# Two transformer blocks on one core: dilated masks added by VectorE with row extremes stored as they come, rope tables computed at FF1's last unit, and the gate stage in another order

## The reference, cut to what matters

```python
# first layer, second half
h = rmsnorm(x, g_pre_mlp)
ff = square(relu(h @ w_ff1)) @ w_ff2             # 1024 -> 4096 -> 1024
x = x + rmsnorm(ff, g_post_mlp)
# second layer
h = rmsnorm_2(x, norm1_g); proj = h @ w_in
for g, (window, dilation) in enumerate(((128, 1), (512, 4), (2048, 16))):
    q, k = partial_rope(q_g, positions), partial_rope(k_g, positions)
    # rope: x1*cos - x2*sin, x2*cos + x1*sin on 16 of 64 features
    s = (q * 64**-0.5) @ k.T  within a residue class, own and previous 128 rows
    s = where(mask, s, -inf)
    m = max(s); p = exp(s - m); den = sum(p)
    lse = m + log(den); o = (p @ v) / den
alpha = softmax(stack(lse)); attn = sum(alpha * outs)
z = gelu(uv); u, v = split(z); v = layernorm(v, ln_g, ln_b)
sgu = u * (tril(w_s) @ v + b_s)                  # per chunk of 128 rows, 8 groups
merged = gate_a * (attn @ w_proj_attn) + gate_b * (sgu @ w_proj_sgu)
x = x + merged @ w_out                           # then norm, gated feed-forward, norm
```

## Time and profile before

| what | value |
|---|---|
| device time, median of 3 runs | 3655.24 us (3654.55 to 3655.67) |
| profiled execution, its own time | 3656.55 us |
| its span | 3654.6 us |
| PE busy | 3512.3 us (96%) |
| PE weight loads (beside it) | 2903.1 us (79%) |
| DVE busy | 1421.5 us (39%) |
| POOL busy | 987.5 us (27%) |
| ACT busy | 933.8 us (26%) |

### The profile page before, as it was taken

The page is one execution under the profiler, slowest core; times in us unless marked ns, Lnnn a source line. Parts: engine busy times, 40 slices in busy tenths (PEclk is TensorE's granted clock), DMA queues, the critical chain, the costliest instruction groups (busy, mean ns, idle before and its releaser), DMA issues.

```text
span 3654.6 us, 44410 instructions
## 1 busy us (share of the span) xinstructions
PE 3512.3 (96%) x17467; PEld 2903.1 (79%) x17467; DVE 1421.5 (39%) x2268; ACT 933.8 (26%) x1575; POOL 987.5 (27%) x429
## 2 busy tenths in 40 slices
PE   7899999999998999999799999998999999999999
PEld 6688877888776888888678888887787778888887
DVE  6882452123345333333644455444113213122234
ACT  4233443312242111111333333333322221111112
POOL 1452102223214333333312222211323122332322
PEclk9999999999999999999999999999999999999999
DMA  4232012212221111111221212213122111111111
GB/s 130 59 85 85 19 52 72 66 52 75 104 81 52 46 57 46 46 46 46 69 85 47 64 46 64 65 45 110 52 75 98 46 52 47 46 56 47 46 46 58
DMA packets 203977, 226.86 MB, mean 62 GB/s; under 512 B 19224, under 2 KB 177604, under 8 KB 203340
## 3 DMA queue, kind: packets, MB, share of 16 engines
q1 hardware_dynamic: 178556, 169.85, 15.3%
q10 hardware_dynamic: 20912, 44.54, 3.5%
q0 software_dynamic: 4384, 10.74, 0.8%
HBM read 191.30 MB, written 31.69 MB: 61 GB/s over the span
## 4 chain that ended last, share of the span: by engine, by line
PE 86%; DVE 5%; issue 5%; POOL 2%; ACT 1%; DMA 0%; ACTq 0%; SPq 0%; DVEq 0%; POOLq 0%
PE ps L274 18%; PE ps L319 16%; PE ps L301 13%; PE ps L302 13%; PE ps L295 12%; PE ps L724 4%; PE ps L2639 2%; PE ps L2610 1%; POOL wlo L266 1%; PE ps L335 1%; PE ps L2627 1%; PE ps L2123 1%; DVE big L470 1%; PE ps L2104 1%; PE ps L500 1%
## 5 line engine op out<-in xcount | busy, mean ns | idle before, releaser
L266 POOL TENSOR_TENSOR wlo<-raw,whi 128x2048 fp32r<-128x2048 f32 (+1 forms) x162 | 700.6, 4325 | 1748.0 <-ACT whi L258 1747.2
L301 PE MATMUL ps<-h_lo,whi 128*128 128x512 f32 x1856 | 723.5, 390 | 2.1 <-POOL wlo L266 2.0
L302 PE MATMUL ps<-h_hi,wlo 128*128 128x512 f32 x1856 | 723.0, 390 | 0.0
L258 ACT ACTIVATE whi<-raw 128x2048 fp32r<-128x2048 f32 (+1 forms) x162 | 288.4, 1780 | 962.0 <-PE ps L295 597.8
L295 PE MATMUL ps<-h_hi,whi 128*128 128x512 f32 x1856 | 462.1, 391 | 9.1 <-DVE gu L2783 5.3
L295 PEld LDWEIGHTS ps<-h_hi,whi 128*128 128x128 f32 x1856 | 349.6, 189 | 83.0 <-issue 9.7
L301 PEld LDWEIGHTS ps<-h_lo,whi 128*128 128x128 f32 x1856 | 349.3, 188 | 76.0 <-POOL wlo L266 3.3
L302 PEld LDWEIGHTS ps<-h_hi,wlo 128*128 128x128 f32 x1856 | 349.0, 188 | 72.5
L1047 DVE TENSOR_TENSOR big<-big,ps 128x512 f32<-128x512 f32 x432 | 295.8, 687 | 252.1 <-PE ps L274 251.9
L274 PE MATMUL ps<-whi,f_hi 128*128 128x512 f32 x864 | 338.3, 392 | 21.8 <-POOL wlo L266 12.4
L319 PE MATMUL ps<-h_lo,whi 128*128 128x512 f32 x880 | 353.1, 401 | 3.9 <-POOL wlo L266 3.9
(11 more groups left out here) (330 smaller groups left out, 4613.1 us busy)
## 6 DMA issues: line engine op xcount, KB each, us to landing
raw<-in_w_ff_dram SPq DMA_DIRECT2D x32, 1024.0 KB, 5.2
raw<-in_w_in_dram SPq DMA_DIRECT2D x57, 512.0 KB, 4.6
raw<-in_w_in_dram SPq DMA_DIRECT2D x28, 1024.0 KB, 5.3
raw<-in_w_ffn_gate_dram SPq DMA_DIRECT2D x11, 1024.0 KB, 5.3
raw<-in_w_ffn_up_dram SPq DMA_DIRECT2D x11, 1024.0 KB, 5.2
raw<-in_w_ffn_down_dram SPq DMA_DIRECT2D x11, 1024.0 KB, 4.9
yt<-y_keep ACTq DMA_DIRECT2D x20, 512.0 KB, 3.9
raw<-in_w_out_dram SPq DMA_DIRECT2D x8, 1024.0 KB, 5.0
```

The costliest lines, as they stand in the source:

```text
L258: nc.scalar.activation(whi[c % 2][:, 0:cols], raw[c % 2][:, 0:cols], ACT.Copy).then_inc(s_hi.sem, 1)
L266: nc.gpsimd.tensor_tensor(wlo[c % 2][:, 0:cols], raw[c % 2][:, 0:cols], whi[c % 2][:, 0:cols].bitcast(F32), ALU.subtract).then_inc(s_lo.se ...
L301: nc.tensor.matmul(ps[:, bank + n, :], w(0, k, m * P, P), src[1][:, k, sl], start=False, stop=False)
L302: last = nc.tensor.matmul(ps[:, bank + n, :], w(1, k, m * P, P), src[0][:, k, sl], start=False, stop=k == ks - 1)
```

## The change: what it does, and the diff

**Masks.** The mask matmuls leave `score`; q is scaled by -0.125, so PSUM holds the negated scores. DVE's `top` runs one `tensor_tensor_reduce` for each head: it adds the mask (now +1e30 where it hides, plain fp32 in `mask_p`) to the scores, writes the sums to `PB2` in SBUF, and leaves their row minimum in `OS`. ACT's `exps` works in place on `PB2` with scale -1 and that minimum as bias, and waits for the heads one by one. PE's next `score` into the same bank waits for DVE's pass and not for ACT's. The copy of the maxima (L2509) is gone; the stored extremes are negated maxima, so `pair_largest` takes minima and subtracts the other way round. The waits for a free `PB2` and a free `OS` go from ACT to DVE.

**Rope tables.** They are made at chunk c = 14 of FF1: on DVE ahead of ups(15), on ACT behind ups(15).

**Gate stage.** DVE masks `wsp` behind the statistics and the addition of eps, and copies `wspT` behind the normalization. PE turns `wsp` behind the fourth tile of the first unit, and does the mixing products behind the second and third tile of the second unit. PE's part of the second `Merge` begins when the gelu tiles, the last pair's features and the eight bias additions are done (`banks_free`), not when the products with `gu` are.

```diff
@@ Dilated.exps (ACT) @@
-                    if 8 * i + b >= 2:
-                        e.wait_ge(p_turned.sem, self.t + 8 * i + b - 1)
-                    e.wait_ge(maxima.sem, self.m + 8 * i + b + 1)
                     for h in range(2):
+                        e.wait_ge(maxima.sem, self.m + 16 * i + 2 * b + h + 1)
                         last = nc.scalar.activation(
-                            PB2[:, b % 2, h, lo:256], ps[:, 2 + 2 * (b % 2) + h, lo:256],
-                            ACT.Exp, bias=mx2[:, i % 2, 2 * b + h:2 * b + h + 1], accum_out=OS[:, i % 2, b, h, HD:HD + 1])
+                            PB2[:, b % 2, h, lo:256], PB2[:, b % 2, h, lo:256], ACT.Exp, scale=-1.0,
+                            bias=OS[:, i % 2, b, h, HD + 1:HD + 2], accum_out=OS[:, i % 2, b, h, HD:HD + 1])
@@ Dilated.top, rows (DVE) @@
-                    e.wait_ge(scores.sem, self.s + 2 * (8 * i + b + 1))
-                    nc.vector.tensor_reduce(mx2[:, i % 2, 2 * b:2 * b + 2], ps[:, 2 + 2 * (b % 2):4 + 2 * (b % 2), lo:256],
-                                            AX, ALU.max, negate=True).then_inc(maxima.sem, 1)
+                    if 8 * i + b >= 2:
+                        e.wait_ge(p_turned.sem, self.t + 8 * i + b - 1)
...
+                    for h in range(2):
+                        e.wait_ge(scores.sem, self.s + 2 * (8 * i + b) + h + 1)
+                        nc.vector.tensor_tensor_reduce(PB2[:, b % 2, h, lo:256], ps[:, 2 + 2 * (b % 2) + h, lo:256],
+                                                       even if self.dil(i) == 8 else band[:, lo:256], 1.0, 3.0e38, ALU.add, ALU.min,
+                                                       OS[:, i % 2, b, h, HD + 1:HD + 2]).then_inc(maxima.sem, 1)
                 def rows(i, b):
-                    e.wait_ge(probs.sem, self.p + 8 * i + b + 1)
-                    nc.vector.tensor_scalar(OS[:, i % 2, b, :, HD + 1:HD + 2], mx2[:, i % 2, 2 * b:2 * b + 2].unsqueeze(2), -1.0,
-                                            None, ALU.mult)
@@ Dilated.score (PE) @@
                     if 8 * i + b >= 2:
-                        e.wait_ge(probs.sem, self.p + 8 * i + b - 1)
+                        e.wait_ge(maxima.sem, self.m + 2 * (8 * i + b) - 2)
...
                     for h in range(2):
-                        nc.tensor.matmul(o[h], ident_r, even_r if self.dil(i) == 8 else band_r[:, lo:256], start=True, stop=False)
-                    for h in range(2):
-                        last = nc.tensor.matmul(o[h], QR[d[h], i % 2, q], KR[d[h], i % 2, k], start=False, stop=True)
+                        last = nc.tensor.matmul(o[h], QR[d[h], i % 2, q], KR[d[h], i % 2, k], start=True, stop=True)
@@ FeedForward.slots @@
-                if after_first is not None and not self.onto_x:
-                    after_first(e)
...
                     if c + 1 < n:
+                        last = tables is not None and not self.onto_x and c + 2 == n
+                        if last and not behind:
+                            tables(e)
                         ups(c + 1, None, us[:-1])
+                        if last and behind:
+                            tables(e)
                         down(c, None, us[-1])
@@ Merge.pe @@
-                self.begin(e, stores=False)
+                if self.banks_free is None:
+                    self.begin(e, stores=False)
+                else:
+                    self.banks_free(e)
@@ SpatialGate @@
+            def banks_free(self, e):
+                e.wait_ge(act_a.sem, self.aa + 16)
+                e.wait_ge(ct_taken.sem, self.dilated.ctk + 8)
+                e.wait_ge(dv.sem, self.mixed + 8)
@@ SpatialGate.pe @@
                 def turn_mixing(n):
-                    if n != 1:
+                    if n != 3:
                         return
...
                 def mixed(n):
-                    if n % 2:
-                        for c in range(2 * n - 2, 2 * n + 2):
+                    if n in (1, 2):
+                        for c in range(4 * n - 4, 4 * n):
                             mix(c)
```

More of the change, by code:

```diff
@@ L182, in hybrid_kernel @@
         YC = phase([("below_yc", [P, 8, 512], F32), ("YC", [P, L], F32)])[1]
-        (gv, XC, ct, cw, QR, KR, VF, PB2, V2, PT2, rt, rp, OS, mx2, mask_r) = phase(kept + [
+        (gv, XC, ct, cw, QR, KR, VF, PB2, V2, PT2, rt, rp, OS, mask_p) = phase(kept + [
             ("QR", [P, 2, L], F32), ("KR", [P, 2, L], F32),
@@ L735, in hybrid_kernel, with __init__ @@
         class Merge(Stage):
-            def __init__(self, w_in, gate_col, w_branch, bias):
+            def __init__(self, w_in, gate_col, w_branch, bias, banks_free=None):
                 super().__init__()
+                self.banks_free = banks_free
                 self.w_in, self.gate_col, self.wb, self.bias = w_in, gate_col, w_branch, bias
@@ L874, in units_of, with slots @@
                 return [unit_no(first + j, i, per) for j in range(self.g + 1)]
-            def slots(self, e, ups, down, after_first=None):
+            def slots(self, e, ups, down, tables=None, behind=False):
                 n = self.n
                 ups(0, None, [unit_no(self.u + j) for j in range(self.g)])
-                if after_first is not None and not self.onto_x:
-                    after_first(e)
                 pairs = (n - 1) // 2
@@ L949, in down @@
                     split_hi(e, (u[0] + 1,) + u[1:])
-                self.slots(e, ups, down, self.rope_act)
+                self.slots(e, ups, down, self.rope_act, behind=True)
                 for t in range(8):
@@ L2176, in __init__ @@
                 self.vf, self.vt = v_feat.take(2 * n), v_taken.take(2 * n)
-                self.s, self.m, self.p = scores.take(16 * n), maxima.take(8 * n), probs.take(8 * n)
+                self.s, self.m, self.p = scores.take(16 * n), maxima.take(16 * n), probs.take(8 * n)
                 self.t, self.pt = p_turned.take(8 * n), p_taken.take(8 * n)
@@ L2341, in act @@
                 self.begin(e)
-                nc.scalar.activation(mask_r[:, :], cst[:, 0:4 * P], ACT.Copy).then_inc(mask_made.sem, 1)
+                nc.scalar.activation(mask_p[:, :], cst[:, P:4 * P], ACT.Copy, scale=-1.0).then_inc(mask_made.sem, 1)
                 def split_qk(i):
@@ L2481, in rotate @@
                                              ).then_inc(rot.sem, 1)
[L2482 removed]
+                    nc.vector.scalar_tensor_tensor(out=rt[:, :], in0=ps[:, bank, :], scalar=(-0.125, 1.0)[k],
                                                    in1=COSR[:, half * HALF:(half + 1) * HALF],
@@ L2489, in rotate_end @@
                     e.wait_ge(rot.sem, d + 1)
-                    nc.vector.scalar_tensor_tensor(out=rp[:, :], in0=rp[:, :], scalar=(0.125, 1.0)[k],
+                    nc.vector.scalar_tensor_tensor(out=rp[:, :], in0=rp[:, :], scalar=(-0.125, 1.0)[k],
                                                    in1=SINR[:, half * HALF:(half + 1) * HALF],
@@ L2755, in dve @@
                 nc.vector.tensor_scalar(mv[:, :, 2:3], mv[:, :, 1:2], EPS, None, ALU.add).then_inc(dv.sem, 1)
-                e.wait_ge(pe_s.sem, self.s + 2)
-                nc.vector.tensor_copy(wspT[:, :, :], ps[:, 4:6, :].rearrange("p b (g n) -> p (b g) n", n=P)).then_inc(dv.sem, 1)
+                e.wait_ge(d_tab.sem, self.tab + 16 * 11)
+                nc.vector.tensor_tensor(wsp[:, :, :], wsp[:, :, :], tril.unsqueeze(1).to_broadcast([P, 8, P]), ALU.mult
+                                        ).then_inc(dv.sem, 1)
                 e.wait_ge(ac.sem, self.c + 1)
@@ L2768, in dve @@
                                                        op0=ALU.mult, op1=ALU.add).then_inc(dv.sem, 1)
+                e.wait_ge(pe_s.sem, self.s + 2)
+                nc.vector.tensor_copy(wspT[:, :, :], ps[:, 4:6, :].rearrange("p b (g n) -> p (b g) n", n=P)).then_inc(dv.sem, 1)
                 dil.pair_largest(e, 3)
@@ L2843, in hybrid_kernel @@
         dilated = add(Dilated(ff.rows))
-        add(SpatialGate(dilated))
-        merge = add(Merge(A["w_in_2"][0], [O2_GA, O2_GB], [A["w_proj_attn_2"][0], A["w_proj_sgu_2"][0]], None))
+        spatial = add(SpatialGate(dilated))
+        merge = add(Merge(A["w_in_2"][0], [O2_GA, O2_GB], [A["w_proj_attn_2"][0], A["w_proj_sgu_2"][0]], None, spatial.banks_free))
         mixed = add(Out(A["w_out_2"][0], merge, Rows("sum", V_NORM + 5 * KT)))
```

27 lines of the change are left out of this document (13 added, 14 removed).

## The result

The changed kernel takes 3620.22 us in the median (3618.88 to 3621.53, 4 runs) beside 3654.89 us before; the ratio is 0.9908, 95% interval 0.9896 to 0.9921. It is faster by 34.7 us, where 52.3 were forecast. The profiled execution took 3620.06 us, 36.5 less than the one before.

A forecast was written before the change was run, and what follows sets the result against it. PE, busy 96% of the span, was taken to bound the kernel, with order of steps deciding at FF1's start and the gate stage. 36.2 + 14.0 + 2.1 = 52.3 us off 3655.24 gave 3603 us, range 3593 to 3616.

The forecast's parts named there:

- slower rival: Dilated stage: POOL's splits hold DVE's new pass, 24 hits of 2.5 us, 60 us slower, 3663 us; chance 0.03.
- Part 1: Dilated stage: 192 mask products leave PE, 36.2 us gained, bounds 16.1 and 42.8; DVE and ACT cost nothing.
- 44 x 0.41 + 52 x 0.35 = 36.2 us: Dilated stage: 44 wide and 52 narrow mask pairs, each priced from its start to the next products' start.
- sum of 52.3: Whole kernel: 36.2 us from the masks, 14.0 from the rope tables and 2.1 from the gate stage.
- what would show it: Signs in the new profile, among them an unchanged distance from the score's predecessor and a stage 36 us shorter.
- lower bound of 16.1 us: Masks: only the columns' streaming comes back, 0.23 us for a wide pair and 0.115 for a narrow one.
- first rival: Masks: only column streaming returns, neighbours' weight loads being hidden under them; 16.1 for 36.2, 3623 us; chance 0.09.
- Part 2: FF1: PE's 12.4 us wait at down(0) and 2.1 us of slow clock go; 14.0 us gained, bounds 10 and 14.5.
- Part 3: Gate stage and merge: the store of gu is issued 2.1 us earlier, 2.1 us gained, bounds -1 and 5.5.
- new wait of the second mixing group: Gate stage: PE's second mixing group waits 2.4 us for the first bias addition.
- 29.8 us behind the store: Merge: its second unit waits for gu to be stored, loaded, rounded and split, 29.8 us behind the store.
- bound of -1: Gate stage, lower bound in us: the new wait brings a slow clock for the last tile.

The follow-up runs named there:

- doubled mask: The kernel before with the mask added twice by PE, 96 more pairs of mask products: 3679.79 us, ratio 1.0070.
- gate_only: The kernel before with only the gate stage's new order and the early start of Merge: 3653.79 us, ratio 0.9999.
- after_again: The changed kernel run once more, unaltered, as the base for the experiments beside it: 3619.52 us, ratio 0.9906.
- begin_back: The changed kernel with PE's part of the merge beginning as before, when all products with gu are made: 3620.97 us, ratio 0.9909.
- early store: The changed kernel with gu stored in two pieces, three quarters ahead of the last gelu: 3615.2 us, ratio 0.9892.

## Why the prediction was wrong

**Which views, and what bounds the kernel: right.** PE's own work counts in the dilated stage. DVE and ACT were covered, as put at nothing: PE's waits for ACT's `VF`, `V` and `YC` there are 2.8, 1.2 and 1.4 us before and 3.3, 1.2 and 1.2 after. DVE's new pass was 0.42 us for a wide block (forecast 0.40) with a maximum of 0.427, so POOL never held it, and the slower rival is out.

**Part 1, the masks: this step failed.** The mechanism was right, the size was not. The term 44 x 0.41 + 52 x 0.35 = 36.2 us measured 21.8 in the traces and 21.1 alone. That is 14.4 of the 15.9 us by which the traces fall short of the sum of 52.3. The step that failed is the sentence "in a stage without idle time the distance of the starts is what the pair takes from the others". The distance from the pair's start to the next start holds two things, the pair and the step from it to its neighbour, and only the first goes with the pair. The doubled mask separates them: 0.23 and 0.24 us of pair, 0.12 and 0.17 us of step, 22.5 and 13.7 us in all. By my own "what would show it", the distance from the score's predecessor to the score should have stayed the same without the pair; it grew by 0.12 us behind the values' product and 0.17 to 0.18 behind a turning, 13.9 us in all. The lower bound of 16.1 us came from the streaming of the columns. It fits wide blocks (0.23 against 0.24 us) and was below the truth for narrow ones, whose pair costs 0.23 us and not 0.115. The first rival named the right side (3623 us, chance 0.09) for a different reason: not that the weight loads were hidden under the masks, but that the score's own load begins no earlier than its product, whatever stands ahead of it. That 3623 lies so near to the measured 3620.2 is partly luck: its 16.1 us for the masks are 5.7 too few, and the gate stage was put 3.3 too high. How much of the step is the load and how much something else is open beyond the 0.09 us that goes with the height.

**The rule weighed there.** The Trainium skill's isolated gap ("TensorE: Matmul & The Clock Gate", Back-to-back issue gap) gave 15.4 us for the 192 products. The doubled mask shows 22.5 us, between the rule and my figure and nearer to the rule: 0.12 us for a product of 256 columns, where the rule has 0.109, and 0.115 for one of 128, where it has 0.056.

**Part 2, the rope tables: right.** Forecast 14.0, measured 14.8 less the first mask pair's 0.35 in the traces and 14.7 alone (interval of the ratio: 8.4 to 18.3 us). The low part of the weight was ready at 1124.67 (forecast 1124.3), and the eight steps at chunk 14 cost nothing, though one of them, held by POOL's split, took 4.98 us instead of 0.69.

**Part 3, the gate stage: right up to the store, wrong behind it.** The wait for `wsp` is 7.67 us (forecast 7.4), the new wait of the second mixing group 1.52 (2.4), the store comes 2.0 us earlier (2.1). The step that failed is "29.8 us behind the store": it took 33.2 (31.2 to 32.9 in the traces of `gate_only`, `after_again` and `begin_back`), because I had carried over the chain with its DMA times and had not asked what the store now meets. The change had brought it to within 0.45 us of the other store. The early store gives 4.3 us back, which shows it. The stretch lost 1.2 us in the traces, just outside the bound of -1. The Trainium skill's rule on the shared ports ("SBUF — State Buffer", Who interferes with whom) was borne out: eps was held until the end of POOL's split again (2466.00 + 3.42 = 2469.42, split until 2469.39).

**The range** of 3593 to 3616 has an upper end that no sum of the prediction gives. The lower bounds of the three parts, 16.1 + 10 - 1 = 25.1 us, would have put it at 3630, and 3620.2 lies inside that. The masks were 36.2 of the sum's 52.3 us with a lower bound of 16.1, and no row showed the stream without them; a bound so far off should have set the range's end.

## What to carry to other kernels

To price an instruction in a full stream by the distance of the starts, take it between two of its own kind, or against a stretch where its neighbours meet without it; the distance to the next kind holds the step between the kinds, and that stays. Products of different heights are worth grouping: making one visit of two saved 0.25 us each time here, after what new waits took back, which is the price of a pair of mask products. When a store is moved, look at which other transfer it now stands beside, and at who waits for the later of the two.

## What the runs showed of the hardware that I had not expected

- Where a score of 64-row products stands right behind 128-row ones, PE's distance to it is 0.12 us (behind the values' product) or 0.17 to 0.18 us (behind a turning) longer than the distance to a mask product was. 0.09 us of that goes when the score has 128 rows; the rest is open. The weight load of the first 64-row product begins with the product and not under its predecessor. One visit fewer saves 0.25 us.
- A second pair of fp32r products of 128 columns costs 0.23 us, nearly the same as one of 256 columns (0.24 us).
- A store of 512 KB from POOL's queue, issued 0.45 us behind one of 2 MB from ACT's, lands after 9.3 us (7.1 to 9.3 in the traces with that order); 3.6 us ahead of it, after 2.9 us; behind the same 2 MB in two pieces of 1.5 and 0.5 MB, issued 3.2 and 0.44 us ahead of it, after 4.6 us.
